# Where two weight buffers begin in SBUF: 384 unused bytes in front of them, 128 behind

## What is computed

```python
q, k, v, gate = jnp.split(h @ w_in, 4, axis=-1)              # 2048 -> 8192, 528 tokens
...
return x + o @ w_out                                         # 2048 -> 2048
...
q, gate = jnp.split(rms_norm(x, norm_g) @ w_in, 2, axis=-1)  # 2048 -> 4096
...
 sgu_u, sgu_v, sgu_g) = jnp.split(h @ w_in[l], IN_OFFSETS, axis=-1)   # 2048 -> 7184, 512 tokens
...
x = x + (mix * gate) @ w_out[l]
x = x + memory_cross_attention(rmsnorm(x, norm_xattn[l]), rmsnorm(mem, norm_mem[l]),
                               w_xq[l], w_xkv[l], w_xo[l])
```

## Time and profile before

| | |
|---|---|
| median of 3 runs | 2866.44 us (2866.18 to 2867.0) |
| the profiled execution, its own time | 2866.59 us |
| its span, first to last instruction | 2864.8 us |
| TensorE matmuls, busy | 2824.8 us, 99% (16,928 instructions) |
| TensorE weight loads, busy | 2442.3 us, 85% |
| VectorE, GpSimd, ScalarE busy | 1244.1, 1166.4, 976.8 us |
| DMA, mean rate | 86 GB/s |

### The profile page before, as it was taken

One profiled execution on the slowest core, in us unless ns is written; L12 is line 12 of the kernel. 1 busy time (PEld: TensorE's weight loads), 2 busy tenths in 40 slices (PEclk: granted clock), 3 DMA queues, 4 the chain that ended last, 5 costly groups with the idle time before them and its releaser, 6 DMA issues.

```text
span 2864.8 us, 41154 instructions
## 1 busy us (share of the span) xinstructions
PE 2824.8 (99%) x16928; PEld 2442.3 (85%) x16928; DVE 1244.1 (43%) x2202; ACT 976.8 (34%) x1433; POOL 1166.4 (41%) x888
## 2 busy tenths in 40 slices
PE   8999999999999999999999999999999999999997
PEld 8999999999999999777877778878778787787775
DVE  6333333433343358353434352723323244455646
ACT  4323222222323244344233344532323333234442
POOL 4333433334333435333434337434344343445442
PEclk9999999999999999999999999999999999999998
DMA  4122222222222212222222234222222222222222
GB/s 184 70 89 74 89 75 74 79 85 74 86 77 75 88 69 89 89 74 74 89 74 75 88 110 148 89 74 89 87 76 88 86 77 76 101 81 89 89 89 74
DMA packets 37084, 247.68 MB, mean 86 GB/s; under 512 B 3985, under 2 KB 4130, under 8 KB 8354
## 3 DMA queue, kind: packets, MB, share of 16 engines
q1 hardware_dynamic: 35728, 241.36, 23.7%
q10 hardware_dynamic: 1170, 3.70, 0.4%
HBM read 240.85 MB, written 4.19 MB: 86 GB/s over the span
## 4 chain that ended last, share of the span: by engine, by line
PE 90%; DVE 4%; ACT 2%; DMA 1%; DVEq 1%; POOL 1%; issue 0%; ACTq 0%; SPq 0%
PE pj L301 20%; PE pj L307 20%; PE pj L305 20%; PE pj L362 3%; PE pj L366 3%; PE pj L364 3%; PE pj L1138 2%; PE pj L1140 2%; PE pj L1139 2%; PE pa L508 1%; PE pa L545 1%; POOL wl L2273 1%; PE pa L1069 1%; DMA raw<-in_stream 1%; PE pa L1493 1%; PE pa L1475 1%
## 5 line engine op out<-in xcount | busy, mean ns | idle before, releaser
L2273 POOL TENSOR_TENSOR wl<-raw,wh 128x512 fp32r<-128x512 f32 x884 | 1166.2, 1351 | 1663.1 <-ACT wh L273 1663.0
L301 PE MATMUL pj<-xh,wh 128*128 128x264 f32 (+2 forms) x3728 | 1079.9, 336 | 3.5 <-POOL wl L2273 2.3
L307 PE MATMUL pj<-xh,wl 128*128 128x264 f32 (+2 forms) x3728 | 1047.4, 327 | 0.0
L305 PE MATMUL pj<-xl,wh 128*128 128x264 f32 (+2 forms) x3728 | 1045.6, 327 | 0.0
L273 ACT ACTIVATE wh<-raw 128x2048 fp32r<-128x2048 f32 x221 | 423.1, 1914 | 972.0 <-PE pj L307 620.7
L301 PEld LDWEIGHTS pj<-xh,wh 128*128 128x128 f32 x3728 | 632.4, 189 | 76.9 <-issue 19.8
L305 PEld LDWEIGHTS pj<-xl,wh 128*128 128x128 f32 x3728 | 631.3, 188 | 59.9 <-issue 5.3
L307 PEld LDWEIGHTS pj<-xh,wl 128*128 128x128 f32 x3728 | 631.3, 188 | 59.6
L388 DVE TENSOR_TENSOR acc<-pj,acc 128x528 f32<-128x528 f32 (+1 forms) x192 | 134.2, 700 | 126.7 <-PE pj L366 125.6
L362 PE MATMUL pj<-oh,wh 128*128 128x264 f32 (+1 forms) x640 | 180.1, 330 | 2.4 <-DVE acc L388 1.3
L366 PE MATMUL pj<-oh,wl 128*128 128x264 f32 (+1 forms) x640 | 177.7, 326 | 0.0
(11 more groups left out here) (317 smaller groups left out, 2726.9 us busy)
## 6 DMA issues: line engine op xcount, KB each, us to landing
raw<-in_stream SPq DMA_DIRECT2D x221, 1024.0 KB, 4.8
acc<-in_x SPq DMA_DIRECT2D x8, 528.0 KB, 10.1
out_y<-acc SPq DMA_DIRECT2D x8, 512.0 KB, 2.9
arena<-in_mem ACTq DMA_DIRECT2D x2, 1024.0 KB, 6.6
cst<-in_cst SPq DMA_DIRECT2D x1, 448.0 KB, 13.4
cos<-in_cos_a SPq DMA_DIRECT2D x1, 264.0 KB, 13.5
sin<-in_sin_a SPq DMA_DIRECT2D x1, 264.0 KB, 13.7
cos<-in_cos_b ACTq DMA_DIRECT2D x1, 264.0 KB, 2.6
```

The costliest lines, as they stand in the source:

```text
L301: pe.matmul(pj[:, pu, b, 0:m], whk, xh[:, k, a:a + m], start=(k == 0), stop=False)
L305: pe.matmul(pj[:, pu, b, 0:m], whk, xl[:, k, a:a + m], start=False, stop=False)
L307: ins = pe.matmul(pj[:, pu, b, 0:m], wlk, xh[:, k, a:a + m], start=False, stop=(k == KD - 1))
L2273: pool.tensor_tensor(wl[:, j, at], raw[:, j, at], wh[:, j, at].bitcast(F32), ALU.subtract).then_inc(s_part if c < LO_PARTS - 1 else s_lo, 1)
```

## The change

Two tensors that nothing reads or writes are allocated, 96 and 32 float32 columns in each partition:

```diff
         raw = as3(sb("raw", 2 * WCOLS)[:, :], 2)
+        sb("gap_w", 96)
         wh = as3(sb("wh", 2 * WCOLS, F32R)[:, :], 2)
         wl = as3(sb("wl", 2 * WCOLS, F32R)[:, :], 2)
+        sb("gap_o", 32)
         oh_all = sb("oh", 4 * T, F32R)
         ol_all = sb("ol", 4 * T, F32R)
```

## The result

The changed kernel takes 2893.23 us (median of 4 runs, 2892.33 to 2893.89), the kernel before 2866.45. The ratio is 1.0092, with a 95% interval of 1.0079 to 1.0104: slower by 26.8 us, where no difference was forecast and the range ended at 2876.

A forecast was written before the change was run, and what follows sets the result against it. The prediction took TensorE's step from one matmul to the next as the bound; four terms of 0 added to the profiled kernel's time gave 2866.4 us, with a range of 2857 to 2876.

The forecast's parts named there:

- What bounds the kernel: TensorE, busy 99%: 13,968 matmuls with `wh` and `wl` take 2342 us, 82% of the span; one cycle each is 5.8 us.
- Step 1: TensorE's weight loads from `wh` and `wl`: no longer straddling a 512-byte boundary saves 0 ns.
- the argument from L508: L508's weights at residues 0 and 384 load in 186/188/193 ns, like those at 128, so no gain from residue.
- Step 2: Distance between TensorE matmuls: 13.3 ns (32 cycles) beyond the columns, a fixed price at either width; change 0.
- rival A: Straddled fp32r loads cause the excess: faster, 2722 us if nearly all goes, 2855 to 2860 for one or two cycles; 13%.
- Step 3: Addresses of weights against moving operand in TensorE: offset costs nothing, 0, with plus or minus 6 us for the 264-column form.
- Rival B: TensorE's two reads collide in the 512-column form at offset 128: up to 3 ns a matmul, 18 us slower, 2884.7 us; 11%.
- Step 4: ScalarE's copy into `wh` and GpSimd's subtraction into `wl`: 0, with 1 us both ways.
- The bound of 7 us: The forecast's own range: 6 us for phase in the 264-column form with 1 us of GpSimd, plus or minus.

The follow-up runs named there:

- the first experiment: 384 unused bytes in front of `xh` in the kernel before, so weights and everything TensorE streams move together to residue 0 (`ol` 256): 2866.32 us, ratio 0.9999.

## Why the prediction was wrong

- **What bounds the kernel**: right, though the sum is short. The trace has 8064 of the 264-column matmuls with these weights instead of 7488, besides the 6192 of 512 columns: 14,640 in all and some 85% of the span at the same rates. One number decides, the step from a matmul to the next, and a cycle of it is 0.2% of the time. The loss is 12 cycles (5.05 ns) on 5899 steps of the 512-column form, 29.8 us, less 4 us that other steps gave back.
- **Step 1, the load itself, 0**: right. Loads from `wh` by the first product take 186/188/193 ns at either residue, and the first experiment shows that residue 0 is free when all is moved. So was the argument from L508.
- **Step 2, the fixed 13.3 ns**: its 0 was right, its reason only in part. No layout went below 226.7 ns in the 512-column form, and the first experiment, without any straddling, speaks against rival A. But a fixed price per matmul at any width it is not: in the 256-column form the run at distance 64 had a projection at 113.3 ns, an excess of 6.6 ns over its columns' 106.7 instead of 13.3. No run shows what the 32 cycles are spent on.
- **Step 3, weights against moving operand, 0**: this is the step that failed. "An offset of 256 bytes costs nothing" was true, but it was an offset of 0 modulo the period, so it said nothing on 128. For 128 I turned to the 264-column form, which goes through all distances at a mean of 122 ns, and concluded that no distance costs much. What the runs showed in its place: going from distance 0 to 128 cost the 512-column form 5.8 ns a matmul. A form that meets many distances in either layout can't show that: the sum of the 264-column form did not change. And the width counts: the 256-column form, at a constant distance like the 512-column one, was 1.2 ns *quicker* at 128 than at 0 in two of its three undisturbed projections. And the rows that I merged by pairs (0.23 to 0.25 us) hide single steps of 115 to 131 ns in the trace: a sign, perhaps, that alignment does something, which I read as noise around a mean.
- **Rival B** named the cause, the place and the sign: weights and moving operand 128 bytes apart, in the 512-column form. That the two reads collide in the memory is its picture of how, which no run shows directly. Its price of 3 ns came from those same pairs; measured were 5.8 ns in undisturbed projections and 5.05 on average. With the 3 ns it said 2884.7 instead of 2893.2, and at a chance of 11% it was underrated. The Trainium skill, "SBUF — State Buffer", section "Who interferes with whom", gives TensorE two independent read ports, one for the moving operand and one for the loads. If independent means that the address of one read doesn't matter to the other, the experiments disagree: the address of the streamed operand relative to the weights moves the step by 6 ns, in projections in which TensorE waits for no other engine, and the measurement decides.
- **Step 4, the writers**: right. GpSimd's median went from 1290 to 1291 ns, and the run with `raw` moved alone shows no change.
- **The bound of 7 us** was the spread of a form (264 columns) whose distances change anyway. For the form in which *every* matmul has the same distance, nothing averages, and the range had to hold B's whole price. Even B's own 2884.7 lay outside it.

## What to carry to other kernels

Where TensorE is the bound and each matmul loads new weights, the address of the stationary block relative to the streamed row is a parameter of its own: here 0 modulo 256 bytes was free in the 512-column fp32r form, and every other distance tried (multiples of 32) cost 2 to 7 ns of 227. Aligning one of the two buffers "to be safe" can break an alignment that both shared by accident; move them together, and look at the step between matmuls, not at the load's duration. A rate from one width or from a mixture of distances says nothing about another width at a fixed distance.

## What the runs showed of the hardware that I had not expected

- The step of the 512-column fp32r matmuls depends on the distance between weights and streamed row: 226.7 ns at 0 and 256 bytes, 233.3 at 32, 64 and 224, 232.5 at 128, 228.9 at 192, while the median recorded duration of a load was 188 ns before and after. The time appears as a later start of the next matmul.
- With one of the three products' weights displaced (`wl`), two steps of three grow, to 232.5 and 234.2 ns. With one stream displaced, the same addresses ran at 233.3 ns in one stretch, all three steps longer, and at 229.0 in another, only the displaced one longer. The cause of either is open.
- The 256-column form runs at 120.0 ns at distance 0, at 118.8 at 128 and at 113.3 to 117.8 at 64: what helps one width hurts another.
